# Differential heads: rotated tiles transposed before the split, and low key halves laid over zeros

## The reference, cut to what matters

```python
h = rmsnorm(x, attn_norm[l])
proj = einsum('bsd,de->bse', h, w_in[l])
sb_q, sb_k, sb_v, df_q, df_k, df_v = split(proj, ...)       # 512 wide each
# stick-breaking: 8 heads of 64: z = q k^T / 8, weights from log-sigmoids and a reversed cumulative sum
# differential: 4 heads, each with two query/key maps of 64 and a value of 128
dq = rope(df_q.reshape(B, S, 4, 2, 64), pos)                # x*cos + rot(x)*sin, tokens x 64
dk = rope(df_k.reshape(B, S, 4, 2, 64), pos)
p = softmax(where(allowed, dq @ dk^T / 8, neg))             # for each of the two maps
attn = p[:, :, 0] - lam * p[:, :, 1]
df = rmsnorm(attn @ df_v, subln_norm[l]) * (1 - lambda_init)
x = x + concat([sb, df]) @ w_o[l]
x = x + square(relu(rmsnorm(x, mlp_norm[l]) @ w_ff1[l])) @ w_ff2[l]
```

## Time and profile before

| | us |
|---|---|
| median of 3 runs | 2010.79 |
| lowest, highest | 2001.95, 2014.46 |
| the profiled execution | 2007.94 |
| its span in the trace | 2006.0 |

### The profile page before, as it was taken

The page is one execution under the profiler, slowest core; times in us unless marked ns, Lnnn a source line. Parts: engine busy times, 40 slices in busy tenths (PEclk is TensorE's granted clock), DMA queues, the critical chain, the costliest instruction groups (busy, mean ns, idle before and its releaser), DMA issues.

```text
span 2006.0 us, 24838 instructions
## 1 busy us (share of the span) xinstructions
PE 1960.5 (98%) x9970; PEld 1643.3 (82%) x9970; DVE 998.1 (50%) x1607; ACT 772.9 (39%) x1358; POOL 265.3 (13%) x354
## 2 busy tenths in 40 slices
PE   9999999999999999999899999999999899999998
PEld 7887887888888888887788888888888688888887
DVE  5658678432233357487552233337678752223334
ACT  4222566332223235366332332225356633233222
POOL 3133244000000001010011220001000102121000
PEclk9999899999999999999999999999999999999999
DMA  7211301133333231221133332332221123333331
GB/s 237 66 53 32 126 22 32 53 116 99 100 95 95 94 95 43 84 85 43 45 103 98 102 95 94 95 96 75 63 85 43 43 94 105 97 95 95 95 102 56
DMA packets 97138, 167.79 MB, mean 84 GB/s; under 512 B 8160, under 2 KB 49152, under 8 KB 97024
## 3 DMA queue, kind: packets, MB, share of 16 engines
q1 hardware_dynamic: 97024, 166.21, 26.7%
HBM read 164.09 MB, written 2.10 MB: 83 GB/s over the span
## 4 chain that ended last, share of the span: by engine, by line
PE 89%; DVE 7%; ACT 2%; issue 1%; POOL 1%; DMA 0%; SPq 0%; DVEq 0%; POOLq 0%; ACTq 0%
PE ps L49 85%; PE ps L52 4%; DVE wlo L71 1%; DVE p L91 1%; ACT p L62 1%; DVE hTl L71 0%; DVE small L82 0%; DVE p L71 0%; DVE t1l L71 0%; DMA raw<-in_w_in_dram 0%; ACT t1h L65 0%; DVE x L71 0%; ACT sk1h L65 0%; DVE t L68 0%; ACT htmB L62 0%
## 5 line engine op out<-in xcount | busy, mean ns | idle before, releaser
L65 ACT ACTIVATE whi<-raw 128x1024 fp32r<-128x1024 f32 x294 | 309.4, 1054 | 713.5 <-PE ps L49 710.5
L71 DVE TENSOR_TENSOR wlo<-raw,whi 128x1024 fp32r<-128x1024 f32 x294 | 361.6, 1231 | 417.8 <-ACT whi L65 416.1
L49 PE MATMUL ps<-hTh,whi 128*128 128x512 f32 (+1 forms) x1176 | 442.4, 376 | 0.0
L49 PE MATMUL ps<-hTh,wlo 128*128 128x512 f32 (+1 forms) x1176 | 437.7, 372 | 0.0
L49 PE MATMUL ps<-hTl,whi 128*128 128x512 f32 (+1 forms) x1176 | 437.5, 372 | 0.0
L49 PE MATMUL ps<-whi,uh 128*128 128x512 f32 x688 | 268.0, 390 | 0.0
L49 PE MATMUL ps<-whi,ul 128*128 128x512 f32 x688 | 267.7, 389 | 0.0
L49 PE MATMUL ps<-wlo,uh 128*128 128x512 f32 x688 | 267.6, 389 | 0.0
L49 PEld LDWEIGHTS ps<-hTh,wlo 128*128 128x128 f32 x1176 | 220.8, 188 | 39.3
L49 PEld LDWEIGHTS ps<-hTl,whi 128*128 128x128 f32 x1176 | 221.0, 188 | 37.2
L49 PEld LDWEIGHTS ps<-hTh,whi 128*128 128x128 f32 x1176 | 220.9, 188 | 37.1
(11 more groups left out here) (242 smaller groups left out, 2228.3 us busy)
## 6 DMA issues: line engine op xcount, KB each, us to landing
raw<-in_w_ff_dram SPq DMA_DIRECT2D x128, 512.0 KB, 3.7
raw<-in_w_gate_up_dram SPq DMA_DIRECT2D x88, 256.0 KB, 3.1
raw<-in_w_in_dram SPq DMA_DIRECT2D x40, 512.0 KB, 4.4
raw<-in_w_in_dram SPq DMA_DIRECT2D x68, 256.0 KB, 3.1
raw<-in_w_down_dram SPq DMA_DIRECT2D x22, 512.0 KB, 3.6
raw<-in_w_o_dram SPq DMA_DIRECT2D x16, 512.0 KB, 4.3
x<-in_x_dram SPq DMA_DIRECT2D x8, 512.0 KB, 6.8
raw<-in_w_out_dram SPq DMA_DIRECT2D x8, 512.0 KB, 4.7
```

The source lines that it names most:

```text
L49: return self.eng.matmul(out, l, r, start=start, stop=stop, skip_group_check=True)
L65: return self.eng.activation(out, in_, ACT.Copy)
L71: return self.eng.tensor_tensor(out, a, b, op)
```

## The change

The rotated tiles of a half stay in fp32 in four buffers (`rot`), one for each token tile. When all four are there, TensorE transposes them unsplit: for each of four feature tiles, four 128x128 blocks (one from each token tile) into one bank, with the fp32 identity. The bank then has the shape of a stick-breaking feature tile, and both kinds are split by the same two new functions, `split_feat` on ScalarE and `split_low` on VectorE. The tiles sg and their ScalarE, VectorE and GpSimd steps are gone. The logits of a differential half wait for all four feature tiles. The low key is no longer written twice: partitions 64 to 127 of kl hold zeros, which GpSimd fills for both halves once a layer, so the product of low query and low key is dropped. The planned costs and orders follow.

```diff
-    ro, rp = (r.t("ro%d" % i, [128, 512]) for i in range(2))
+    rp, rot0 = r.t("rp", [128, 512]), r.t("rot0", [128, 512])
-    sg = [r.t("sg2%s" % n, [128, 4, 128], F32R) for n in ("q", "h", "l")]
+    rot = [rot0] + [r.t("rot%d" % i, [128, 512]) for i in range(1, 4)]
...
-                P.add(("sgh", k), "ACT", dA(256) + dA(512), ...)
-                P.add(("sgq", k), "POOL", 0.8, ("sgh", k))
-                P.add(("sgk", k), "DVE", dV(512), ("sgh", k), pri=2)
-                for e in range(3):
-                    P.add(("skt", k + (e,)), "PE", 0.35, ...)
+                P.add(("evV", (m, "D%d" % half, i)), "DVE", 3 * dV(512) + 0.1, last, ("nrm", (key, 3)), ("skt", (m, 0, 3)) if half else None, seq="rope", pri=2)
+                P.add(("skt", k), "PE", 0.44, ("evV", (m, "D%d" % half, 3)), seq="skt", pri=2, take=[("T", [("evV", (m, "D%dt" % half, i))])])
+                P.add(("sSa", (m, "D%dt" % half, i)), "ACT", (2 if i < 2 else 4) * dA(512), ("skt", k), seq="skA", pri=2)
+                P.add(("evV", (m, "D%dt" % half, i)), "DVE", 2 * dV(512), ("sSa", (m, "D%dt" % half, i)), seq="skV", pri=2)
-                P.add(("evV", (m, name, i)), "DVE", (2 if i < 2 else 4) * dV(512) - (0 if i < 2 else 0.5), ("sSa", (m, name, i)), pri=2)
+                P.add(("evV", (m, name, i)), "DVE", 2 * dV(512), ("sSa", (m, name, i)), pri=2)
...
-                    P.add(("fsq", (m, half, qi)), "ACT", dA(256), fin, P.last.get("fr"), seq="lfA", pri=3)
-                    P.add(("fr", (m, half, qi)), "DVE", dV(256), ("fsq", (m, half, qi)), seq="fr", pri=3)
+                    P.add(("fsq", (m, half, qi)), "ACT", dA(256), fin, seq="lfA", pri=3)
+                    P.add(("fr", (m, half, qi)), "DVE", dV(256), ("fsq", (m, half, qi)), seq="lfV", pri=3)
-                    P.add(("fD", (m, half, qi)), "DVE", 0.54, ("rs", (m, half, qi)), pri=3)
+                    P.add(("fD", (m, half, qi)), "DVE", 0.54, ("rs", (m, half, qi)), seq="lfV", pri=3)
...
+                    pe.wait_ge(*at("rop", (m, half, 3)))
+                    for t in range(4):
+                        ins = pe.tr(ps[b][:, 128 * t:128 * t + 128], rot[t][:, 128 * f:128 * f + 128], ident[:, :])
+                    ins.then_inc(*up("skt", (m, half, f)))
...
-                        pe.wait_ge(*at("skA", (m, half, qi, 2)))
-                        pe.wait_ge(*at("skV", (m, half, qi, 1)))
+                        for f in range(4):
+                            pe.wait_ge(*at("evV", (m, "D%dt" % half, f)))
...
+        def split_feat(m, name, half, i, b):
+            q_, kh, kl = stk[half]
+            for e in range(2):
+                h = 2 * (i % 2) + e
+                src = ps[b][64 * e:64 * e + 64, :]
+                if i < 2:
+                    act.copyA(q_[0:64, h, :], src).then_inc(*up("sSa", (m, name, i, e)))
+                else:
+                    act.copyA(kh[0:64, h, :], src)
+                    act.copyA(kh[64:128, h, :], src).then_inc(*up("sSa", (m, name, i, e)))
...
+        def split_low(m, name, half, i, b):
+            q_, kh, kl = stk[half]
+            for e in range(2):
+                h = 2 * (i % 2) + e
+                s = ps[b][64 * e:64 * e + 64, :]
+                dve.wait_ge(*at("sSa", (m, name, i, e)))
+                if i < 2:
+                    ins = dve.tt(q_[64:128, h, :], s, f32(q_[0:64, h, :]), ALU.subtract)
+                else:
+                    dve.wait_ge(*at("kz", m))
+                    ins = dve.tt(kl[0:64, h, :], s, f32(kh[0:64, h, :]), ALU.subtract)
+            ins.then_inc(*up("evV", (m, name, i)))
...
+        def key_zeros(m):
+
+            yield T["in", (m, "D0", 0, 0)]
+            pool.wait_ge(*at("ul", (m - 1, NK[m - 1] - 1)))
+            for half in range(2):
+                ins = pool.fill(f32(stk[half][2][:, :, :]), 0.0)
+            ins.then_inc(*up("kz", m))
```

More of the change, by code:

```diff
@@ L723, in plan_late @@
                     k = (m, i, r_)
-                    P.add(("llg", k), "PE", 0.09 + len(maps) * 2 * (N / 2400 + 0.014), *[("skA", (m, half, t, 2)) for t in range(qi + 1)], *[("skV", (m, half, t, 1)) for t in range(qi + 1)],
+                    P.add(("llg", k), "PE", 0.09 + len(maps) * 2 * (N / 2400 + 0.014), *[("evV", (m, "D%dt" % half, f)) for f in range(4)],
                           seq="llg", pri=3, take=[("L", [("lex", k)])])
@@ L1345, in stack @@
             for half in range(2):
[L1346 to L1357, removed]
+                for f in range(4):
+                    yield T["skt", (m, half, f)]
+                    b, before = tring.take(("evV", (m, "D%dt" % half, f)))
+                    for done in before:
+                        pe.wait_ge(*at(*done))
+                    bank_of["sk", m, half, f] = b
+                    pe.wait_ge(*at("rop", (m, half, 3)))
+                    for t in range(4):
+                        ins = pe.tr(ps[b][:, 128 * t:128 * t + 128], rot[t][:, 128 * f:128 * f + 128], ident[:, :])
+                    ins.then_inc(*up("skt", (m, half, f)))
         def late_logits(m):
@@ L1686, in evac2 @@
                 half = int(name[1])
-                q_, kh, kl = stk[half]
                 act.wait_ge(*at("llg", (m, LAST_D[half], 1)))
                 act.wait_ge(*at("mm", ("in", m, name, i, 3)))
[L1690 to L1697, removed]
+                split_feat(m, name, half, i, b)
@@ L1710, in stack_copy @@
-        def stack_copy(m):
-            for half in range(2):
-                for t in range(4):
-                    for i in (0, 2):
-                        yield T["skA", (m, half, t, i)]
-                        act.wait_ge(*at("skt", (m, half, t, i)))
-                        act.copyA(stk[half][i][:, :, 128 * t:128 * t + 128],
-                                  ps[bank("sk", m, half, t, i)][:, :].rearrange("p (k n) -> p k n", k=4)).then_inc(*up("skA", (m, half, t, i)))
+                for f in range(4):
+                    yield T["sSa", (m, "D%dt" % half, f)]
+                    act.wait_ge(*at("skt", (m, half, f)))
+                    split_feat(m, "D%dt" % half, half, f, bank("sk", m, half, f))
@@ L2202, in stack @@
         def stack(m):
             for half in range(2):
-                for t in range(4):
-                    yield T["sgk", (m, half, t)]
-                    src = ro[:, :].rearrange("p (h d) -> p h d", h=8)
-                    def dup(ap):
-                        return ap.rearrange("p h (e d) -> p h e d", e=2)
-                    dve.wait_ge(*at("sgh", (m, half, t)))
-                    dve.tt(dup(sg[2][:, :, :]), bc(src[:, 4:8, :], 2, [128, 4, 2, 64]), f32(dup(sg[1][:, :, :])), ALU.subtract).then_inc(*up("sgk", (m, half, t)))
@@ L2213, in stack_copy @@
-        def stack_copy(m):
-            for half in range(2):
-                for t in range(4):
-                    yield T["skV", (m, half, t, 1)]
-                    dve.wait_ge(*at("skt", (m, half, t, 1)))
-                    dve.copyV(stk[half][1][:, :, 128 * t:128 * t + 128],
-                              ps[bank("sk", m, half, t, 1)][:, :].rearrange("p (k n) -> p k n", k=4)).then_inc(*up("skV", (m, half, t, 1)))
+                for f in range(4):
+                    yield T["evV", (m, "D%dt" % half, f)]
+                    split_low(m, "D%dt" % half, half, f, bank("sk", m, half, f))
```

48 lines of the change are left out of this document (8 added, 40 removed).

## The result

The kernel after took 1983.55 us (median of 4 runs, 1976.41 to 1985.79), the kernel before beside it 2012.59 us (4 runs, 2001.95 to 2014.46). The ratio is 0.986, 95% interval 0.982 to 0.990. The forecast was 2000 with a range of 1992 to 2014, so it was wrong: the change gave nearly three times what the sum said, 29 us between the medians against 9.9.

A forecast was written before the change was run, and what follows sets the result against it. Bound: the tensor engine up to 935 us of the first attention layer, then the chain to the stick-breaking logits. Terms -10.6 - 0.9 + 1.6 = -9.9 us took the median from 2010.79 to 2000.9, stated as 2000; range 1992 to 2014.

The forecast's parts named there:

- Transposes: Tensor engine, rotated tiles: 48 old groups go, 16 fp32 groups come; net 10.6 us less, bounds 7.2 to 12.0.
- The rule of four passes: Rival, new transpose groups: true FP32 takes four passes, so transposes lose 2.5 us; time 2011, chance 0.03.
- The shorter wait: After the last projection tile: without the doubling, the 3.34 us wait shrinks by 0.46 us, 0.9 in two layers.
- Zeros: GpSimd, each layer: two fills, at most 2.1 us each, hidden in idle time before the last inverse root; cost zero.
- Reordering: Differential halves: low planned costs make the tensor engine wait for splits, 0.4 us a half; +1.6 us, between 0 and 5.
- The late half delays the tail: Rival, second differential half: later logits push vector work into the layer's tail; +10 us, about 2020, chance 0.15.
- The clock stays up: Rival, wait at 935 us: the shorter wait no longer lowers the clock; 3.4 us a layer back, 1993, chance 0.07.

The follow-up runs named there:

- the two sets: Seven kernels with new transpose groups and eight with old: tensor-engine stream without pauses and clock loss averaged 606.8 and 611.9 us a layer against 611.9 and 617.2.
- Doubled: The kernel before with every old transpose group issued twice, order unchanged: 2023.3 us, ratio 1.007 to the kernel before.
- the tripled kernel: The kernel after with every new transpose group issued three times, order unchanged: 1987.6 us, ratio 0.990 to the kernel before.
- the order held: The kernel before with low keys over zeros and every planned cost as before, so the order stays: 2010.05 us, ratio 1.0006.
- the four orders run on its instructions: The kernel before (2008 to 2013 us) and three versions with planned costs changed and no instruction: 1997.34, 1988.85 and 1994.98 us.
- the late start alone: The kernel before, except that the logits of a differential half wait for all four token tiles: 1993.18 us, ratio 0.993.
- the filled wait: The kernel before with 30 identity transposes ahead of the last half's first logits, where TensorE waits: 2007.37 us, ratio 1.000.

## Why the prediction was wrong

**Transposes: right.** -10.6 us forecast; the ledger's rest gives -11.3 for the pair of profiles and about -10 for the two sets. Counted from the layer's start, the last matmul of the input projection starts 6.7 us earlier in the first layer, where I had said 5. The new group costs 0.36 + 0.08 us in its row, against 0.45. Doubled and tripled groups give 0.30 and 0.39 us, without most of the restart. The rule of four passes (the Trainium skill, FP8 and Floating Point Precision, TensorE Precision Notes) would have made the tripled kernel some 16 x 1.2 = 19 us a layer longer by my working from the earlier trace rows; it was 6.1 and 3.4. For transposes of this form that rival is refuted.

**The shorter wait: right in its place, not to be found in the time.** With the order held the wait was 2.88 us, as forecast, and the time 1.0006 (0.998 to 1.003), which would not show 0.9 us; in the profiled execution the clock behind it took more than that back. I had added 0.9 us to the sum as if nothing behind a wait could take it back.

**Zeros: right.** 1.82 us a fill, and no cost was seen: the inverse root behind them still found its engine idle.

**Reordering: the step that failed.** I put it at +1.6 us, between 0 and +5, looking only at waits that the new steps would add. Those I found about where I looked: 0.52 and 0.39 us ahead of rotated transposes and 0.67 ahead of the first logits of half 1, 1.6 us in the first layer, twice the 0.8 of my term. In place of the +1.6 (and the -0.9 of the shorter wait) the pair of profiles shows about -15 us: pauses fell by 9.9 us and the clock's loss by 5.2 in two layers. For the same diff changes planned costs and dependences, and the list scheduler then places all of the layer's steps anew. One planned cost of this diff, alone and on the old instructions, gave 12 us. The order that the kernel before happened to have was an unlucky one: of the four orders run on its instructions it is the slowest, by 12 to 22 us. No bound below zero stood in that term, though nothing in the profile excluded a gain: 11.6 us of pauses and 5.2 us of clock in a layer were there to be won, and the tail's nine pauses were in the timeline that I read for the wait. Instead of one term of +1.6 it should have been a spread of some 10 us to either side (my estimate from the 23 us between the orders), with the pauses and the clock's loss of before as the most it could give.

**The late half delays the tail: the mechanism came, with the other sign.** First logits of half 1 came at 865.56 - 2.6 = 863.0, where I had put them at 863. Its last came at 890.1, just at the point from which I said it decides. Yet the next half started at 892.5 instead of 896.01, and work left for the wait made the tail shorter. Before, TensorE's last product of half 0 starts at 930.56, three input projection chunks follow in a row, and behind them, from 935.58, it has four transposes to do and then stands still for 3.34 us. After, its last projection matmul starts at 931.21, and one product and four transposes stand behind it:

```profile
932.08 1.16 PE L49 MATMUL ps<-t,vS 128*128 128x128 f32 x8 [0.26 <-DVE t L68]
933.07 0.38 PE L52 MATMUL ps<-ident,mixR 128*128 128x128 f32 x2
```

By the last product with the values 7 tiles of the output projection are done instead of 5. I had priced the vector work that moves into the tail, not the TensorE work that moves into its gap. The kernel with the late start alone, on old transposes, showed the sign by itself: 17 us faster.

**The clock stays up: partly so.** Its loss fell from 5.2 to 1.8 and 3.4 us a layer, at a remaining wait of 1.47 us (my 2.9 was the wait with the order held). Its price was wrong too: I took all of the low stretch at the wait for lost time, but the filled wait cut the loss of the second layer by 3.5 us and left its length as it was.

What stays open: which swap of steps closes which pause, and how much of the clock's share in the ledger was lost time. I compared the sums and the ends of stages, not the orders step by step.

## What to carry to other kernels

Where a static planner sets the order, a diff in its costs is a change of its own. Give it a range on both sides, as wide as the pauses and the low clock in the trace allow, and measure it by a kernel with the planned numbers changed and the instructions left alone. Before crediting a change with its time, compare it with before under more than one such number, and price instructions by repeating them in place, where the order is held. The cheapest gain here was not in the diff: 0.2 us in one planned cost gave 9.5 us between the medians, 7 by the ratios.

## What the runs showed of the hardware

Filling a wait did not pay. In the first layer 3.44 us of fill moved the stretch at 1.2 GHz from 940 to 945 us, onto dearer matmuls, with pauses of 0.63, 0.49 and 1.13 us ahead of it. In the second only 3.4 us at the lower level were left of 10.2, and the layer was as long as before.

Transposes held the clock up meanwhile. After the empty wait the granted clock was 0.50 in 940 to 945 us. After the same wait filled with transposes it was 0.96. The Trainium skill (TensorE: Matmul & The Clock Gate, Part 4: PE-mode transpose) says that full clock doesn't engage for transposes. These rows disagree as far as keeping the full clock goes; whether transposes alone would raise it, no run here shows.

The clock's share also shows between runs of one kernel. Of the 18 executions of the kernel before beside the first experiments, the five of 2000 to 2003 us had a mean granted clock of 0.993 to 0.997, and the three slowest, 2011.81 to 2014.42 us, one of 0.987 to 0.989. The gap is about 0.7% or 15 us, against a spread of 14.
